# The DeltaNet rows' convolution and SiLU in the input projection, and the FFN's closing inside the FFN program

## The reference

```python
for layer in range(2):
    mod = silu(c) @ ada_w[layer] + ada_b[layer]          # 6 vectors, for the latent and for the context tokens
    h = rms_norm(x, norm_pre_mix) * (1 + mod[1]) + mod[0]
    p = h @ w_in[layer]                                  # 3344 columns, split among four mixers
    o = concat(gdn(p), global_gqa(p), window_gqa(p), hgrn(p)) @ w_out[layer]
    x = x + mod[2] * rms_norm(o, norm_post_mix)
    f = conv_ffn(rms_norm(x, norm_pre_ffn) * (1 + mod[4]) + mod[3])
    x = x + mod[5] * rms_norm(f, norm_post_ffn)
return x[latent]

# the gated DeltaNet mixer's rows:
qkv = silu(dwconv_centered(qkv, conv_w))                 # 3 taps along the tokens, per column
q, k, v = split(qkv); q = l2_normalize(q) * 64 ** -0.5; k = l2_normalize(k)
beta = sigmoid(beta_raw); g = -exp(a_log) * softplus(a_raw + dt_bias)
```

## Time and profile before

| | |
|---|---|
| median of 3 runs | 4762.68 us (4760.15 to 4768.19) |
| profiled execution: its time, its span | 4763.57 us, 4760.6 us |
| PE busy | 3919.5 us, 82% |
| weight loads of PE | 3150.5 us, 66% |
| DVE, ACT, POOL busy | 2133.6 us (45%), 1343.8 us (28%), 1150.1 us (24%) |
| mean granted PE clock | 0.907 of full speed |
| DMA | 283.24 MB, mean 59 GB/s |

### The profile page before, as it was taken

The page is one execution under the profiler, slowest core; times in us unless marked ns, Lnnn a source line. Parts: engine busy times, 40 slices in busy tenths (PEclk is TensorE's granted clock), DMA queues, the critical chain, the costliest instruction groups (busy, mean ns, idle before and its releaser), DMA issues. The chain is left out here.

```text
span 4760.6 us, 81723 instructions
## 1 busy us (share of the span) xinstructions
PE 3919.5 (82%) x33438; PEld 3150.5 (66%) x33438; DVE 2133.6 (45%) x2920; ACT 1343.8 (28%) x1879; POOL 1150.1 (24%) x884
## 2 busy tenths in 40 slices
PE   5999559576878999999993999559658888999995
PEld 2888435364767788888882787435437767888884
DVE  3444735465556432332236323735465555332234
ACT  4111333234333321211213211333243334222221
POOL 1000520203531232332321000520205512333322
PEclk8999669797988999999996999669779989999997
DMA  4444110101012111101101234110110021111112
GB/s 164 161 158 157 46 61 0 39 3 35 4 53 85 54 36 38 39 31 40 40 27 62 105 128 142 42 58 1 39 36 4 4 101 59 49 49 44 48 49 88
DMA packets 71558, 283.24 MB, mean 59 GB/s; under 512 B 7392, under 2 KB 12768, under 8 KB 66272
## 3 DMA queue, kind: packets, MB, share of 16 engines
q1 hardware_dynamic: 55136, 198.51, 12.2%
q10 hardware_dynamic: 16128, 80.49, 4.6%
HBM read 223.65 MB, written 47.45 MB: 57 GB/s over the span
## 5 line engine op out<-in xcount | busy, mean ns | idle before, releaser
L3444 DVE SCALAR_TENSOR_TENSOR y<-ps,taps,y 128x1023 f32<-128x1023 f32 (+1 forms) x132 | 134.2, 1016 | 866.2 <-DVEq L3442 859.7
L491 PE MATMUL ps<-h_hi,wu_hi 128*128 128x512 f32 x1680 | 460.4, 372 | 12.3 <-PEq L3344 12.3
L491 PE MATMUL ps<-h_hi,wu_raw_rest 128*128 128x512 f32 x1680 | 459.4, 371 | 0.0
L491 PE MATMUL ps<-h_whole_rest,wu_hi 128*128 128x512 f32 x1680 | 459.0, 371 | 0.0
L3489 POOL TENSOR_TENSOR wu_raw_rest<-wu_raw,wu_hi 128x1024 fp32r<-128x1024 f32 x84 | 201.3, 2397 | 1025.8 <-POOLq L3488 1025.8
L491 PE MATMUL ps<-h_hi,w_hi 128*128 128x512 f32 (+1 forms) x1200 | 314.9, 367 | 39.6 <-PEq L487 39.6
L491 PEld LDWEIGHTS ps<-h_hi,wu_hi 128*128 128x128 f32 x1680 | 294.6, 188 | 69.6 <-issue 13.5
L491 PEld LDWEIGHTS ps<-h_hi,wu_raw_rest 128*128 128x128 f32 x1680 | 294.6, 188 | 56.3
L491 PEld LDWEIGHTS ps<-h_whole_rest,wu_hi 128*128 128x128 f32 x1680 | 294.1, 188 | 56.2
L491 PE MATMUL ps<-h_hi,w_raw_rest 128*128 128x512 f32 (+1 forms) x1200 | 313.1, 365 | 0.0
L491 PE MATMUL ps<-h_whole_rest,w_hi 128*128 128x512 f32 (+1 forms) x1200 | 313.0, 365 | 0.0
(11 more groups left out here) (390 smaller groups left out, 8141.4 us busy)
## 6 DMA issues: line engine op xcount, KB each, us to landing
wu_raw<-in_w_up_dram SPq DMA_DIRECT2D x88, 512.0 KB, 3.3
w_raw<-in_w_in_dram SPq DMA_DIRECT2D x54, 512.0 KB, 4.6
ada_w<-in_ada_rest_dram ACTq DMA_DIRECT2D x27, 1024.0 KB, 6.8
rows<-rows ACTq DMA_DIRECT2D x42, 640.0 KB, 4.9
wd_raw<-in_w_down_dram SPq DMA_DIRECT2D x40, 512.0 KB, 4.2
h_whole<-rows SPq DMA_DIRECT2D x24, 640.0 KB, 6.3
ada_w<-in_ada_rest_dram ACTq DMA_DIRECT2D x27, 512.0 KB, 4.8
raw<-rows SPq DMA_DIRECT2D x20, 640.0 KB, 4.7
```

The costliest lines, as they stand in the source:

```text
L491: mm = pe.matmul(ps[:, lo:lo + width], w[a][:, t, :], rhs[b][:, t, lo:lo + width], start=(t == 0 and i == 0), stop=(t == n_k - 1 and i == 2))
L3444: dve.scalar_tensor_tensor(y[:, s, lo + 1:hi], ps[s][:, lo:hi - 1], k.taps[:, s, 0:1], y[:, s, lo + 1:hi], ALU.mult, ALU.add).then_inc(own ...
```

## The change

- **Start.** SP loads two tiles of `xT` ahead of the modulation weights and six behind them. PE does seven of the eight `ada_products` ahead of the ones product. DVE takes the weights' remainders (`between`) ahead of the modulation.
- **Projection.** The six tiles of the DeltaNet's q, k and v (tiles 10 to 15) are convolved and activated where they come out of PSUM: `collect_conv` and `taps`. The loops around them are cut in three.
- **DeltaNet rows.** One program takes the place of two. It loads finished rows straight into `qkv`; ACT squares q, POOL squares k, and ACT's Ln and Exp of the norms are interleaved with those of the decay.
- **FFN's closing.** `residual_phase` and `store_phase` are gone. Squares and sums follow each output of the last group; the gate is applied by ACT; DVE scales and adds, POOL adds tiles 1, 3 and 5. In layer 0 ACT and PE at once make the row factor that layer 1's projection needs (`k.factor`, at a place that this projection keeps free), whose norm then only scales. In layer 1 each tile is stored when it is closed.

```diff
 load_phase
-                for t in range(KD):
+                for t in range(2):
                     sp.dma_start(k.xT[:, t, :], a["xT"][:, t, :]).then_inc(k.x_tiles[t].sem, 16)
 Norm.sync
         if self.ada is not None:
             self.load_ada(sp, 0)
+            for t in range(2, KD):
+                sp.dma_start(self.k.xT[:, t, :], self.x[:, t, :]).then_inc(self.k.x_tiles[t].sem, 16)
 Norm.scalar
         if self.ada is None:
-            act.preload_act_table_set("natural_log_exp_and_others")
+            between()
+        else:
...
 Norm.tensor
-            self.ada_products(pe, 0, KD // 2)
+            self.ada_products(pe, 0, KD - 1)
 input_projection_phase
+        def taps(dve, s, tile, n):
+            j, x = T_GDN.index(tile), ps[s]
+            first = sum(len(conv_parts(rows_of(t))) for t in range(T_GK, tile))
+            dve.wait_ge(centre_done.sem, centre_done.at(tile - T_GK + 1))
+            for lo, hi in conv_parts(n):
+                dve.scalar_tensor_tensor(out[:, s, lo + 1:hi], x[:, lo:hi - 1], k.vec(V_GCONV + j), out[:, s, lo + 1:hi],
+                                         ALU.mult, ALU.add).then_inc(tap_done.sem, 1)
...
+        def collect_conv(act, s, tile, n, next_item):
...
+            load_item(act, 1 - s, next_item)
...
+            act.activation(out[:, s, 0:n], ps[s][:, 0:n], ACT.Copy, scale=k.vec(V_GCONV + 6 + j)).then_inc(centre_done.sem, 1)
+            round_weights(act, s)
+            act.wait_ge(side_done.sem, side_done.at(sum(len(conv_parts(rows_of(t))) for t in range(T_GK, tile + 1))))
+            act.sem_inc(ps_free[s], 1)
+            act.activation(out[:, s, 0:n], out[:, s, 0:n], ACT.Silu).then_inc(own_a, 1)
...
 vector part of the projection
+                for tile in range(T_GK, T_GQ + 2):
+                    taps(dve, 1 - tile % 2, tile, rows_of(tile))
+                    rest_of_weights(dve, 1 - tile % 2)
+                    vector_item(dve, 1 - tile % 2, tile)
 gdn_rows_phase, scalar
+                for j in range(2):
+                    act.wait_ge(rows_in[j].sem, rows_in[j].at(16))
+                    act.activation(sq[:, j, :], qkv[:, j, :], ACT.Square).then_inc(sq_done.sem, 1)
+                act.wait_ge(gates_in.sem, gates_in.at(16))
...
+                for j in range(4):
+                    act.wait_ge(sums_done.sem, sums_done.at(j + 1))
+                    act.activation(r[j], ps[j % 2][:, 0:T], ACT.Ln, bias=k.eps[:, 0:1]).then_inc(ln_done.sem, 1)
+                    act.wait_ge(ln_done.sem, ln_done.at(j + 1))
+                    act.activation(r[j], r[j], ACT.Exp, scale=-0.5).then_inc(root_done.sem, 1)
+                    if j == 0:
+                        act.wait_ge(less_done.sem, less_done.at(1))
+                        act.activation(soft[g, :], soft[g, :], ACT.Exp).then_inc(exp_done.sem, 1)
...
 mix_out_ffn_phase
+        def close_layer(sp):
+            for t in tiles:
+                sp.dma_start(k.h[:, t, 0:n], k.x_dram[:, t, 0:n]).then_inc(x_back.sem, 16)
+            if layer == DEPTH - 1:
+                for t in tiles:
+                    wait_closed(sp, t)
+                    sp.dma_start(a["out"][:, t, :], k.xT[:, t, 0:SEQ]).then_inc(stored.sem, 16)
...
+        def add_square(dve, o):
...
+            dve.tensor_tensor(facc, facc, y[:, o % 2, 0:n], ALU.add).then_inc(facc_done.sem, 1)
+        by_pool = (1, 3, 5)
+        def close_rows(dve):
...
+            for t in tiles:
+                dve.wait_ge(fmod_done.sem, fmod_done.at(t + 1))
+                dve.tensor_tensor(f[:, t, 0:n], f[:, t, 0:n], froot, ALU.mult).then_inc(fscaled.sem, 1)
+                if t:
+                    close_tile(dve, t - 1)
+            close_tile(dve, KD - 1)
...
 mix_out_ffn_phase, tensor
                 tensor_down(pe, 0, (last_hi, last_lo))
+                pe.wait_ge(facc_done.sem, facc_done.at(KD - 1))
...
+                if layer < DEPTH - 1:
+                    pe.wait_ge(f_done.sem, f_done.at(KD))
+                    for t in tiles:
+                        pe.wait_ge(xsq_done.sem, xsq_done.at(t + 1))
+                        for lo, w in SEGS:
+                            mm = pe.matmul(ps[1][:, lo:lo + w], k.const(C_ONES), y[:, t % 2, lo:lo + w],
+                                           start=(t == 0), stop=(t == KD - 1))
 mix_out_ffn_phase, scalar
+                for o in tiles:
+                    act.wait_ge(f_done.sem, f_done.at(o + 1))
...
+                    act.activation(y[:, o % 2, 0:n] if o else facc, f[:, o, 0:n], ACT.Square).then_inc(fsq_done.sem, 1)
...
+                        ins = act.activation(f[:, o, lo:hi], f[:, o, lo:hi], ACT.Identity, scale=k.mods[:, 5 * KD + o, c:c + 1])
+                act.preload_act_table_set("natural_log_exp_and_others")
...
 build
-                residual_phase(k, k.xT, x, n, 5, reload=k.x_dram)
-        store_phase(k, a)
```

More of the change, by code:

```diff
@@ L387, in vector @@
         k, n, acc, r, own = self.k, self.n, self.acc, self.r, self.own_v
[L388 to L408, removed]
+        if self.ada is not None:
+            for t in range(KD):
+                dve.wait_ge(self.sq_full[t % 2], 1)
+                dve.sem_inc(self.sq_full[t % 2], -1)
+                if t == 0:
+                    ins = dve.tensor_copy(acc[:, 0:n], self.sq[:, 0, 0:n])
+                else:
+                    ins = dve.tensor_tensor(acc[:, 0:n], acc[:, 0:n], self.sq[:, t % 2, 0:n], ALU.add)
+                if t < KD - 2:
+                    ins.then_inc(own, 1)
+                    dve.wait_ge(own, 1)
+                    dve.sem_inc(own, -1)
+                    dve.sem_inc(self.sq_free[t % 2], 1)
+                elif t < KD - 1:
+                    ins.then_inc(own, 1)
+                    dve.wait_ge(own, 1)
+                    dve.sem_inc(own, -1)
+                else:
+                    ins.then_inc(own, 1)
+                    dve.wait_ge(own, 1)
+                    dve.sem_inc(own, -1)
+                    dve.sem_inc(self.acc_pe, 1)
+        between()
         if self.ada is not None:
@@ L559, in vector_item, with rows_of @@
             dve.sem_inc(ada_free[s], 1)
+        def taps(dve, s, tile, n):
[5 more added lines that the diff above has]
+                                         ALU.mult, ALU.add).then_inc(tap_done.sem, 1)
+            for e, (lo, hi) in enumerate(conv_parts(n)):
+                dve.wait_ge(tap_done.sem, tap_done.at(first + e + 1))
+                dve.scalar_tensor_tensor(out[:, s, lo:hi - 1], x[:, lo + 1:hi], k.vec(V_GCONV + 12 + j), out[:, s, lo:hi - 1],
+                                         ALU.mult, ALU.add).then_inc(side_done.sem, 1)
+        def rows_of(tile):
+            return n_own if tile >= T_GQ else T
         def multiply(pe, s, n, ready=None):
@@ L605, in _ @@
             def _(pe):
-                norm.tensor(pe)
+                if layer == 0:
+                    norm.tensor(pe)
                 multiply(pe, 0, T, (norm.even_pe, norm.odd_pe))
@@ L777, in conv_parts @@
+        centre_done.base += 6
+        for m in (tap_done, side_done):
+            m.base += sum(len(conv_parts(rows_of(t))) for t in range(T_GK, T_GQ + 2))
 def conv_parts(n):
     return [(0, SEQ)] + ([(SEQ, n)] if n > SEQ else [])
-class Job:
-    def __init__(self, tile, dest, taps=None, silu=False, width=None, factor=None, rope=False, to_tokens=None):
-        self.tile, self.dest, self.taps, self.silu = tile, dest, taps, silu
-        self.width, self.factor, self.rope, self.to_tokens = width, factor, rope, to_tokens
@@ L3234, in over @@
             return k.nc.alloc_sbuf_tensor_at(f"{name}_{k.count}", shape, dt, offset=offset)
+        factor = k.factor = over("factor", [P, T], k.factor_at)
         mixed = [over("mixed_even", [P, KD, 512], at_g), over("mixed_odd", [P, KD, 256], at_g + 16384)]
@@ L3465, in add @@
                 dve.sem_inc(own["dve"], -1)
+                if last_group and hi == n:
+                    dve.sem_inc(f_done.sem, 1)
             for o in range(KD):
@@ L3557, in _ @@
                 load_last_down(sp)
+                close_layer(sp)
             @block.tensor
```

582 lines of the change are left out of this document (172 added, 410 removed).

## The result

The changed kernel takes 4634.1 us in the median of four runs, the kernel before, beside it, 4765.2: ratio 0.9725, 95% interval 0.9709 to 0.9742, so 131 us faster. The same kernel in a second set of runs: 4618.6 against 4754.9, ratio 0.9709 [0.9693, 0.9725], 136 us faster. The prediction was 4622; the first figure lies 12 us above it, within the stated range, and the forecast gain of 140.5 us compares with 131 and 136.

A forecast was written before the change was run, and what follows sets the result against it. PE bounds projections, mixers and FFN but nearly idles in four stages between; gains there of 17.0 + 75 + 26.9 + 21.6 = 140.5 us off the profiled 4763.57 give 4623.1, as median 4622 us, range 4604 to 4647.

The forecast's parts named there:

- the ones product takes 2.4: Start: PE's ones product over the x tiles' squares takes 2.4 us, then the last eighth 3.4, done at 48.7.
- the start gains half: Start: queues share unevenly, x tiles or eighths come late, PE ends near 56; gain 9 us, 4630; chance 0.12.
- The rival of a bound projection: Projection: DVE or ACT bounds the moved tiles, 12 tiles x 4 us, total 4670; chance 0.05.
- R: FFN's closing: time the rows' factor is ready, forecast E + 10.9 in layer 0 and E + 9.4 in layer 1.
- the rival of a low clock: Closing: PE stays at the low clock in the ones products, 9 us more, 4631; chance 0.17.
- the rival without exclusion: Closings: GpSimd and DVE don't exclude each other, 7 and 6 us less, 4609; chance 0.05.
- E: FFN's closing: end of DVE's last addition of an FFN output; forecast to slip by 0.8 us in layer 1.

The follow-up runs named there:

- the kernel with both parts: DeltaNet rows' part and FFN's closing both put into the kernel before, with or without the start's part; layer 1's mixer stretch 240.8 to 248.0 us.
- The three edits together: Changed kernel with all closing adds on DVE, all eight eighths and copies ahead of the start's sum, 15 unread products before the closing's ones product: 4603.1 us, 0.9665.

## Why the prediction came out as it did

**Start, 17.0 predicted, 14.2 measured, 13.8 as a part alone.** The loads ran as counted: the third x tile is squared at 31.81, and the eighths never starved PE, which began 2 us earlier than reckoned. Two terms of the sum were mis-sized. I let each square and sum follow its tile's arrival; with two buffers between ACT and DVE a tile takes 1.84 us, so the sum ended at 43.84, not 42.5. And I priced the ones product at 2.4 us, what it took in the kernel before, where PE came to it straight from work; behind 4.78 us of idle time its granted clock was 0.58 and it took 4.08. (The terms written down end at 48.3, not 48.7; that slip of 0.4 hid a little of it.) The step "the ones product takes 2.4" is refuted by the row, and the run with all eighths ahead shows it from the other side (2.39 with PE busy until shortly before). The rival "the start gains half" did not occur.

**Rows, 75 predicted, 72.8 measured, 75.2 as a part alone.** The mechanism held: ACT's row sets the end, 13.0 us of it in layer 0. Two terms were small: the first Ln started at 11.7 and 11.6 us, not 10.6, and in layer 1 DVE's decay steps held ACT for 1.1 us, a wait that the prediction named and priced at half (25.8 to 27.2, 26.5 taken). So the stages took 26.9 and 27.8 us. That GpSimd does not lie on the path for its own length was confirmed by taking its squares away, and that the projection pays nothing by its length. The rival of a bound projection did not occur.

**Closing of layer 0, 26.9 predicted, 28.0 measured.** R, DVE's end and the next program came within 0.6 us of the forecast. For R that is partly luck: the terms written down (1.6, 1.8, 4.14, 2.9) add up to 10.4 and not to the 10.9 that was taken, and the single ones product, priced at the low clock's 4.14, took 4.63 at a granted clock of 0.50. The ones products for the next norm did start low and rise: the clock was 0.50 for the first 5.7 us and 1.00 from then on, and the last twelve took 4.56 us, 2.3 for six. So PE did not hold up the end, and the rival of a low clock fell for this stage. GpSimd's adds were priced at 2.5 us each and cost 2.7, while DVE's own operations were priced at 1.43 and start 1.40 apart; without the adds DVE is done 3.9 us sooner in layer 0, so the rival without exclusion fell.

The Trainium skill (SBUF — State Buffer, Who interferes with whom) says that a VectorE instruction with two SBUF inputs contends with a GpSimd one that reads SBUF, and that their shared ports are an exclusive lock. That rule with GpSimd's recorded duration in the kernel before gave R + 29.8, and the trace says R + 26.4. The exclusion is there; what it costs DVE is not GpSimd's recorded 4.0 us but 2.7. The first of the recorded adds starts 1.25 us before DVE's own running add ends (2483.67 against 2484.92) and ends 2.75 us after that, so the record seems to hold GpSimd's own wait; that is inferred from these times and was not tested apart.

The Trainium skill (SBUF — State Buffer, Who interferes with whom) says too that a VectorE copy or tensor_scalar can enter a two-port mode and then contends with GpSimd. The trace agrees: the one-input operation L861 ahead of layer 0's mixer took 2.83 us beside GpSimd's square and 0.82 without it.

**Closing of layer 1, 21.6 predicted, 23.6 measured.** The factor came at E + 8.9, not 9.4, and the last store, at 2.6 us to landing instead of 3.7, let the span end 3.1 us after DVE. Another 0.8 of the 2.0 us is no gain: the prediction took off 0.8 for a later E, which the table's stretch does not contain. E did slip, by 0.6: the last six outputs were added within 14.2 us, before within 13.6. DVE's end at R + 21.3 against 21.4 hides two errors: GpSimd's adds cost 2.1 us each and not 1.9, DVE's operations start 1.14 apart and not 1.21.

**What the sum left out.** The parts add up to 140.1 alone and were predicted at 140.5; in the trace of the whole the four edited stages give 138.6, since the errors (-2.8, -2.2, +1.1, +2.0) nearly cancel. The first comparison gave 131.1, the second 136.3. What the first lacks is, in its profile, layer 1's mixer at 248.0 us where the profile of before had 237.6. The prediction took a stage that is not edited to last as long as before. In fourteen profiles it lasted 236.6 to 248.0 us; the five at a granted clock of 0.96 or 0.97 took 236.6 to 241.4, the seven at 0.95 from 240.5 to 244.5, and the two at 0.94 took 248.0 and 246.1. Two profiles of one kernel differed by 0.9, 3.7 and 4.1 us, so a single pair cannot tell such a stretch to better than some 4 us; whether the other 4 to 6 belong to the kernel with both parts is open. What sets that clock was not found.

## What to carry to other kernels

A stage in which the bounding engine stands still is priced by the longest row of waits within it. Priced one by one, the parts added up to 140 us here, and the whole gave 131 and 136: what an unedited stage does belongs to the error of the sum. Before work is given to GpSimd beside a DVE that is on the path, compare what it takes from DVE (here 1.40 us an add) with what it costs DVE (2.7). Where PE waits for a sum, give it the products that are ready: that fills the idle time, and here it left the clock up for the product that everyone waits for (2.39 us instead of 4.08). The three edits together, on top of the change, took the ratio from 0.9709 to 0.9665 [0.9652, 0.9678].

## What the runs showed that I had not expected

- After 4.78 us of idleness the ones product at the start took 4.08 us for six (granted clock 0.58), after 5.20 us of idleness 4.63 (0.50); after 1.60 and 1.76 us it took 2.39 and 2.42 (1.00). Fifteen products that nobody reads, 3.6 us in all, shortened the two closings by 2.0 and 1.8 us.
- A tensor_scalar of one operand on 8 partitions took 2.83 us instead of 0.82 next to a GpSimd multiplication of 128 partitions.
- Which of two operations starts first, by as little as 0.04 us, decided over the rows' stage: where GpSimd's first square was ahead of DVE's L857 it lasted 27.7 to 28.0 us, else 26.2 to 26.9.
- GpSimd's squares of 128x1280 took 2.39 us each in the earlier trace rows and 3.25 (6.50 for two) beside DVE's decay operations in layer 0.
- A stretch of 7166 matmuls that no edit touches took 236.6 to 248.0 us in fourteen profiles of eleven kernels, with PE's granted clock from 0.94 to 0.97.
